# Long convolution of a two-block model: the first filter products moved to the norm ahead of it, and one residual moved by a weight chunk

## What is computed

```
x = x + gate * y                                   # y: output of the MLA layer
a = modulate(rmsnorm(x, norm_g[1]), shift, scale)  # the norm "n5"
u = depthwise_conv(a @ hy_w_in, hy_conv_w, hy_conv_b)
z, g1, g2 = channels of u
z = g1 * (longconv(z, filter 0) + bias[0] * z)
z = g2 * (longconv(z, filter 1) + bias[1] * z)
x = x + gate * ((z * silu(gate channels)) @ hy_w_out)
```

## Time and profile before

| | |
|---|---|
| three runs | 1974.87, 1975.39, 1976.33 us (median 1975.39) |
| profiled execution | 1977.09 us, its span 1975.3 us |
| granted TensorE clock, mean | 0.991 |
| PE busy | 1917.8 us (97%) |
| DVE busy | 1400.4 us (71%) |
| ACT busy | 833.0 us (42%) |
| POOL busy | 226.7 us (11%) |
| chain that ended last | PE 70%, DVE 19%, ACT 6%, issue 3% |

### The profile page before, as it was taken

How to read it: one execution, slowest core, us unless ns; L and a number is a source line. 1 busy time by engine, 2 the same in 40 slices (tenths; PEclk the granted TensorE clock), 3 DMA queues, 4 the chain that set the end, 5 groups by cost and what they waited for, 6 DMA issues and landing times.

```text
span 1975.3 us, 24342 instructions
## 1 busy us (share of the span) xinstructions
PE 1917.8 (97%) x9606; PEld 1602.5 (81%) x9606; DVE 1400.4 (71%) x2091; ACT 833.0 (42%) x1324; POOL 226.7 (11%) x233
## 2 busy tenths in 40 slices
PE   8999999999999999999999999999999989999997
PEld 6888887778788889888888888778888878788886
DVE  5477766998889678848755874556555568798884
ACT  5233334442233356644323443444434344455442
POOL 2133321002201330010000001100000101010011
PEclk9999999999999999999999999999999989999998
DMA  5212123335544431134443433321111323332421
GB/s 185 75 58 65 54 65 96 138 132 191 201 152 152 142 124 42 45 106 139 149 163 125 144 112 96 107 64 40 36 37 39 114 68 128 91 134 75 150 95 53
DMA packets 60531, 206.55 MB, mean 105 GB/s; under 512 B 6785, under 2 KB 7233, under 8 KB 59265
## 3 DMA queue, kind: packets, MB, share of 16 engines
q1 hardware_dynamic: 52864, 191.36, 29.1%
q10 hardware_dynamic: 7552, 13.64, 2.0%
HBM read 194.48 MB, written 10.49 MB: 104 GB/s over the span
## 4 chain that ended last, share of the span: by engine, by line
PE 70%; DVE 19%; ACT 6%; issue 3%; POOL 1%; DMA 0%; ACTq 0%; DVEq 0%; SPq 0%
PE PS L335 18%; PE PS L339 17%; PE PS L338 17%; DVE wlo L1899 4%; DVE col_f L2140 2%; PE PS L448 2%; PE PS L954 2%; ACT whi L1221 2%; PE PS L342 2%; PE PS L345 1%; PE PS L346 1%; PE PS L746 1%; PE PS L943 1%; DVE q L2062 1%; PE PS L727 1%
## 5 line engine op out<-in xcount | busy, mean ns | idle before, releaser
L335 PE MATMUL PS<-nhi,whi 128*128 128x512 f32 x1456 | 587.8, 404 | 16.3 <-DVE wlo L1899 4.7
L339 PE MATMUL PS<-nhi,wlo 128*128 128x512 f32 x1456 | 570.4, 392 | 0.0
L338 PE MATMUL PS<-nlo,whi 128*128 128x512 f32 x1456 | 569.3, 391 | 0.0
L1899 DVE TENSOR_TENSOR wlo<-raw,whi 128x1024 fp32r<-128x1024 f32 x288 | 362.6, 1269 | 154.2 <-ACT whi L1221 152.9
L1221 ACT ACTIVATE whi<-raw 128x1024 fp32r<-128x1024 f32 x288 | 299.7, 1052 | 167.8 <-PE PS L335 97.8
L335 PEld LDWEIGHTS PS<-nhi,whi 128*128 128x128 f32 x1456 | 275.0, 189 | 78.6 <-issue 9.7
L339 PEld LDWEIGHTS PS<-nhi,wlo 128*128 128x128 f32 x1456 | 274.4, 188 | 59.1
L338 PEld LDWEIGHTS PS<-nlo,whi 128*128 128x128 f32 x1456 | 275.4, 189 | 51.5 <-issue 1.0
L2800 POOL TENSOR_TENSOR diag<-diag,sqb 128x512 f32<-128x512 f32 (+1 forms) x56 | 72.9, 1301 | 758.6 <-ACT sqb L1230 675.8
L335 PE MATMUL PS<-hh_f,whi 128*128 128x512 f32 x352 | 137.2, 390 | 0.0
L339 PE MATMUL PS<-hh_f,wlo 128*128 128x512 f32 x352 | 137.0, 389 | 0.0
(11 more groups left out here) (371 smaller groups left out, 3285.7 us busy)
## 6 DMA issues: line engine op xcount, KB each, us to landing
raw<-in_stream SPq DMA_DIRECT2D x288, 512.0 KB, 3.5
aw_f<-in_ada SPq DMA_DIRECT2D x48, 512.0 KB, 4.5
rows<-sd_f ACTq DMA_DIRECT2D x32, 256.0 KB, 2.3
rows_h<-rows SPq DMA_DIRECT2D x8, 1024.0 KB, 6.3
wd_f<-in_decay ACTq DMA_DIRECT2D x16, 256.0 KB, 3.2
hT<-in_xT SPq DMA_DIRECT2D x8, 256.0 KB, 6.8
out<-hT SPq DMA_DIRECT2D x8, 256.0 KB, 2.0
wd_f<-in_filt_out ACTq DMA_DIRECT2D x8, 128.0 KB, 3.0
```

Source lines behind the costliest of these rows:

```text
L335: op = e.matmul(out, hi, xh, start=first, stop=False)
L338: e.matmul(out, hi, xl, start=False, stop=False)
L339: return e.matmul(out, lo, xh, start=False, stop=last)
L1899: e.tensor_tensor(m.wlo[:, c % HL, :], m.raw[:, c % RAW, :], m.whi[:, c % HL, :].bitcast(F), SUB).then_inc(*s.w_lo.tick(c))
```

## The change

The 18 products of the first six tiles (alternating row, cosine part, sine part of the first filter group) are taken in the norm n5. Six come between the two groups of one-column sums, six between the sums and the spread, six behind the spread. The row and the sine part both use bank 4 now, one after the other, with ACT's copy of the row between them; the cosine part uses bank 5. ACT copies the row behind the root, and the sine and cosine parts at the start of `forward(0)`. The counters on ACT and DVE count the six tiles at the new place. On DVE the residual of tile 7 now stands ahead of the rounding that its loop reaches with the seventh tile.

```diff
@@ summed_late (PE)
         for last, src in enumerate((m.acc, m.sqb[:, 1, :])):
             if last:
+                between()
                 q.wait_ge(*s.sq.at(site, KD - 1))
@@ hyena (PE)
-        summed_late("n5", lambda: q.wait_ge(*s.h.at("mla_out", 0)))
+
+        def first_row():
+            q.wait_ge(*s.h.at("mla_out", 2))
+            q.wait_ge(*s.made_v.at("h_lo", 0, 0, 0))
+            for x in range(2):
+                op = mm_w(B[4], tiles.take([("alt", x, 0)]), a.hh[:, 0, x, :], a.hl[:, 0, x, :], x == 0, x == 1)
+            op.then_inc(*s.filled.tick("alt", 0, 0))
+
+        def first_part(b, key, col, half, rows):
+            for k, x in enumerate(rows):
+                op = mm_w(b, tiles.take([("dft", k, col)]), a.hh[:, half, x, :], a.hl[:, half, x, :], k == 0, k == 1)
+            op.then_inc(*s.filled.tick(key, 0, 0, 0))
+
+        summed_late("n5", lambda: q.wait_ge(*s.h.at("mla_out", 0)), first_row)
+        first_part(B[5], "bk", 0, 0, (0, 1))
         spread("n5")()
+        q.wait_ge(*s.taken_a.at("alt", 0, 0))
+        q.wait_ge(*s.made_v.at("h_lo", 0, 0, 3))
+        first_part(B[4], "bj", 4, 1, (2, 3))
@@ convolve, forward(j) (PE): with j == 0 of the first group "done", its alt and dft products are left out
-                    q.wait_ge(*s.taken_a.at("alt", od, c))
+                    q.wait_ge(*(s.taken_a.at("bj", 0, 0, 0) if done else s.taken_a.at("alt", od, c)))
@@ hyena (ACT)
         root("n5")
+        for _ in range(2):
+            w.tiles(1)
+        q.wait_ge(*s.filled.at("alt", 0, 0))
+        e.activation(a.alt[:, :], B[4], ACT.Copy).then_inc(*s.taken_a.tick("alt", 0, 0))
+        for _ in range(4):
+            w.tiles(1)
@@ convolve, forward(j) (ACT)
+                if done:
+                    q.wait_ge(*s.filled.at("bj", 0, 0, 0))
+                    e.activation(ks[:, 1, :], bu, ACT.Copy).then_inc(*s.taken_a.tick("bj", 0, 0, 0))
                 e.activation(ks[:, 0, :], bk, ACT.Copy).then_inc(*s.taken_a.tick("bk", od, c, j))
@@ mla, last loop (DVE)
-            for k, _ in enumerate(w.steps(KD if i > 3 else 1)):
+            for k, _ in enumerate(w.steps(6 if i == 7 else KD if i > 3 else 1)):
                 if (i, k) in ROWS_AT:
                     next(rows)
             residual(MLA_OUT_BANKS[i], i, ("mla_out",), m.ada[0][:, 16 + i, 0:1])
+        for _ in range(2):
+            w.tiles(1)
@@ hyena (DVE)
         root("n5", m.rc)
+        for _ in range(6):
+            w.tiles(1)
```

More of the change, by code:

```diff
@@ L378, in summed, with summed_late @@
         return sums(site, m.acc, 4, ready)
-    def summed_late(site, free):
+    def summed_late(site, free, between=lambda: None):
         q.wait_ge(*s.acc.at(site, KD - 2))
@@ L1084, in forward @@
                 sums, differences = (0, 1), (2, 3)
-                if j == 0:
+                done = j == 0 and prev is None
+                if j == 0 and not done:
                     for k, x in enumerate(sums):
@@ L1088, in forward @@
                         if k == 0:
-                            q.wait_ge(*(s.taken_v.at("bu", *prev, 3) if prev else s.h.at("mla_out", 1)))
+                            q.wait_ge(*s.taken_v.at("bu", *prev, 3))
                             q.wait_ge(*s.made_v.at("h_lo", od, c, 0))
@@ L1092, in forward @@
                     op.then_inc(*s.filled.tick("alt", od, c))
-                for k, x in enumerate(sums if j < 2 else differences):
+                for k, x in enumerate(() if done else sums if j < 2 else differences):
                     w = tiles.take([("dft", k, j)])
@@ L1098, in forward @@
                         else:
-                            q.wait_ge(*(s.taken_a.at("bk", *prev, 3) if prev else s.h.at("mla_out", 2)))
+                            q.wait_ge(*s.taken_a.at("bk", *prev, 3))
                         q.wait_ge(*(s.made_v.at("hm", od, c) if j else s.made_v.at("h_lo", od, c, 0)))
                     op = mm_w(bk, w, a.hh[:, 0, x, :], a.hl[:, 0, x, :], k == 0, k == 1)
-                op.then_inc(*s.filled.tick("bk", od, c, j))
-                for k, x in enumerate(differences if j < 2 else sums):
+                if not done:
+                    op.then_inc(*s.filled.tick("bk", od, c, j))
+                if j == 0:
+                    q.wait_ge(*s.made_v.at("zt", od, c, 3))
+                for k, x in enumerate(() if done else differences if j < 2 else sums):
                     w = tiles.take([("dft", k, 4 + j)])
                     if k == 0:
-                        q.wait_ge(*(s.taken_a.at("bj", od, c, j - 1) if j else s.made_v.at("zt", od, c, 3)))
+                        if j:
+                            q.wait_ge(*s.taken_a.at("bj", od, c, j - 1))
                         q.wait_ge(*s.made_v.at("h_lo", od, c, 3))
                     op = mm_w(bj, w, a.hh[:, 1, x, :], a.hl[:, 1, x, :], k == 0, k == 1)
-                op.then_inc(*s.filled.tick("bj", od, c, j))
+                if not done:
+                    op.then_inc(*s.filled.tick("bj", od, c, j))
                 even, odd = Z_SIGNS[j]
@@ L1803, in forward @@
                 i = j % 2
-                if j == 0:
+                done = j == 0 and od == 0 and c == 0
+                if j == 0 and not done:
                     for _ in range(2):
@@ L1812, in forward @@
                     e.activation(a.alt[:, :], bu, ACT.Copy).then_inc(*s.taken_a.tick("alt", od, c))
-                w.tiles(1)
-                w.tiles(1)
+                for _ in range(0 if done else 2):
+                    w.tiles(1)
                 q.wait_ge(*s.filled.at("bk", od, c, j))
@@ L1825, in forward @@
                     e.activation(a.hh[0:1, 0, 0, :], a.hm[0:1, :], ACT.Copy).then_inc(*s.made_a.tick("hm", od, c))
-                for _ in range(2):
-                    w.tiles(1)
-                q.wait_ge(*s.filled.at("bj", od, c, j))
-                e.activation(ks[:, 1, :], bj, ACT.Copy).then_inc(*s.taken_a.tick("bj", od, c, j))
+                if not done:
+                    for _ in range(2):
+                        w.tiles(1)
+                    q.wait_ge(*s.filled.at("bj", od, c, j))
+                    e.activation(ks[:, 1, :], bj, ACT.Copy).then_inc(*s.taken_a.tick("bj", od, c, j))
                 for _ in range(Z_TILES[j]):
@@ L2668, in forward @@
                 i = j % 2
+                done = j == 0 and od == 0 and c == 0
                 if j == 0:
-                    for _ in range(4):
+                    for _ in range(0 if done else 4):
                         w.tiles(1)
@@ L2674, in forward @@
                                     SUB).then_inc(*s.made_v.tick("hm", od, c))
-                for _ in range(Z_TILES[j] + (2 if j == 0 else 4)):
+                for _ in range(Z_TILES[j] + (0 if done else 2 if j == 0 else 4)):
                     w.tiles(1)
```

## The result

| | before | changed |
|---|---|---|
| median of 14 runs each, us | 1975.75 | 1971.83 |
| lowest to highest, us | 1973.38 to 1977.18 | 1970.34 to 1973.32 |
| profiled execution, us | 1977.09 (span 1975.3) | 1970.34 (span 1968.5) |
| mean granted clock of that execution | 0.991 | 0.995 |

The ratio is 0.9981, with a 95% interval of 0.9973 to 0.9989: 3.9 us less in the medians, against 3.7 forecast. The changed kernel was run once more, beside two other kernels: 1971.67 (11 runs, before 1975.08 in 17), ratio 0.9979 [0.9970, 0.9987].

What follows compares the result with a forecast made beforehand. TensorE is busy for 97% of the span, so edits pay only where it waits, runs at half clock or ends a chain. 1.62 + 1.37 - 1.13 + 1.85 = 3.7 us, from 1975.39 to 1971.7; range 1969.5 to 1975.0.

Steps and rivals of the forecast that it cites:

- Step 1: On DVE, the last residual goes ahead of a weight chunk, so the square ends 1.15 us earlier.
- Step 2: Six row products between the groups of sums spend the residual's gain but for 0.08 us; root 0.6 us earlier.
- Step 3: Six cosine products between sums and spread, hidden but for 0.03 us; spread takes 1.02, scaled rows start 1.62 us earlier.
- Step 4: Six sine products behind the spread and two ACT copies, all hidden; products end near 1589.0, stream starts at 1590.48.
- Step 5: Start of the projection stream at full clock: nine steps take 1.90 us and not 3.27, 1.37 us gained.
- Step 6: At the turn, one more chunk ahead of DVE's four folds stalls PE's transposes by 1.13 us.
- Step 7: At the convolution's start ACT runs through behind the last column: 1.85 us gained, 0.72 net of the stall.
- B: No stall at the turn: gain 4.8 us, time 1970.6; chance 0.16.
- E: ACT's copies behind the last column do not run through: gain 1.9 us, time 1973.5; chance 0.05.
- C: Clock falls once in the norm, at about 1585, for 3.3 us: gain 2.1 us, time 1973.3; chance 0.16.
- D: Half clock through the whole chain of the norm: 0.4 us slower, time 1975.8; chance 0.06.
- two bounds: Trace before the change: full clock after 2.63 us without products near 1272, half clock following 2.06 us near 1682.

Runs made afterwards that it cites:

- the four edits together: Changed kernel plus a chunk ahead of the first take, ACT's copies ahead of the last, DVE's chunk and row's low half in its wait: 1968.81 us, ratio 0.9966.

## Why the prediction was right

**Step 1, the residual**: 0.43 behind the last MLA product, as forecast (1.15 us). **Step 2**: the square is ready at 1581.50 (1580.87 + 0.63), 1.2 us before the six row products are through, and the second group starts behind them, at 3.02 against 3.04 before. That it spends what step 1 wins is shown from two sides: with the residual alone the sums start at 1.90, and with the products alone the sums don't move (3.04). The group took 0.95 (forecast 1.03), the root came 0.62 earlier (0.6). One reading of this step was wrong: the forecast gives the residual 0.08 us in the change, and it is worth 0.30 at the root and 0.28 at the first multiply, since without it the root follows ACT's table load of 1.28 us, which the forecast does not count. The sum is not touched by it, as in the change the load ends 0.86 ahead of the root. **Step 3**: the cosine products are hidden and the spread takes 1.07 (1.02): 1.57 us for 1.62. **Step 4**: six products and ACT's copy are hidden; PE still has 1.42 idle ahead of the stream (about 1.5). **Step 5**: 1.33 us for 1.37 (the gain at the first take, 2.89, less the 1.56 at the start of the stream).

**Step 6**: PE's idle piece is 0.91, less than the 1.13 forecast, but three of the four transposes stand ahead of it and only the last waits. From the first transpose to the next product it is 1.48 us (1625.87 - 1624.39) against 0.37 before, 1.11 more, and so it is from the first take to the last one (26.86 against 25.75). The term should be read from such distances, not from the idle piece alone. Moving the chunk away gives it back (25.73).

**Step 7**: the multiply comes 4.85 behind the take, forecast 4.95, before 6.80: 1.95 us for 1.85. ACT copies without a pause. PE's wait is 1.94 (1.9), and costs next to nothing in the first multiply: with the copies ahead of the take the wait is gone, and that multiply gains only 0.2.

The sum of the steps is 3.73 at the first multiply, for 3.7. It is that close partly by luck, since the errors of 0.02 to 0.10 have both signs.

**The rivals.** B (no stall) falls by the 1.11 us. E (the copies do not run through) falls by ACT's timeline. C and D (the clock falls in the chain) did not happen in either profile of the change. Here the forecast was right on grounds that were thinner than it made them: it argued from twelve long products and no wait above 1.5 us, and the experiments show how near it was. Its two bounds were single draws. The waits of 2.63 us at 1272 and of 2.06 us at 1682 stand in all thirteen profiles, the first in a part of the program that all kernels share. The first was followed by half clock in five of them, three times with the very next product, as here with the copies ahead of the last take (before: 0.47):

```profile
1275.33 0.77 PE L335 MATMUL PS<-nhi,whi 128*128 128x512 f32 x1 [2.63 <-DVE call L2465]
```

The second was followed by it in eight. So the row at 1275.01 was no bound, and that the clock would stay up in the change did not follow from it. In the norm itself, of all thirteen profiles:

| what stands between the last MLA product and the spread | clock fell in the norm |
|---|---|
| sums and waits only (before, residual alone, all behind the spread) | 3 of 3 profiles |
| six products behind the sums | 2 of 4 |
| six products between the two groups of sums, six behind them | 0 of 6 |

The Trainium skill (TensorE: Matmul & The Clock Gate, "What's actually happening") says that "the default state is throttled, and activity releases the throttle". The traces agree in direction: the more long products in the chain, the rarer the fall, and none where there were twelve. If the order made no difference, three falls among the nine profiles of the first and last row would all be in the first row once in 84 times, so the products probably have a part in it. Whether their number does it or their place between the sums isn't shown: no kernel has six between the sums and none behind. The prediction says that the trace disagrees with the page, since the wait at 1272 did not make the clock fall. That doesn't follow from the sentence quoted, which names no length of a wait, and in five of thirteen profiles it did fall there. The traces also show that D's price is real: in the order with six products behind the sums and a late residual it took the whole gain of the chain and 0.07 us more (8.06 against 7.99). D's chance of 0.06 for the change itself is not contradicted by its two profiles, nor by the four others with six products between the sums.

What the timed runs can settle is less: the ratio of each experiment has an interval of about 0.1% on either side, 2 us. That the change is faster than before, and that the four edits together are faster than before by 0.21 to 0.47%, is shown by times; with the products behind the spread no difference from before is shown (0.9983 to 1.0002). The sizes of single terms are shown by the traces alone.

## What to carry to other kernels

In a chain of short operations on several engines PE's waits can take products that are wanted later; put them where they also end in time at half clock, because a product ahead of a link costs nearly twice as much once the clock has fallen (0.43 against 0.23 us a step here). Take from one trace that a wait can pass at full clock, not that it always will. After moving work out of one place, follow each engine's order to the next place where it has no slack: here the tiles taken ahead brought a chunk in front of the folds (1.1 us), and the copies freed ACT only to leave DVE as the end of the chain. Cost each term from rows of the trace and compare by distances between events, since two executions of the same kernel differ by more than such a change gives (17 of the kernel before: 1972.44 to 1978.77). Look for what runs beside the step that you shorten: here a table load of 1.28 us was hidden until the sums ahead of it got faster.

## What the runs showed of the hardware

- Whether the granted clock falls behind a given wait differs from execution to execution of the same work. Behind 2.63 us without a product (start of the wait near 1272) it fell in 5 of 13 profiles, behind 2.05 to 2.10 us (near 1680) in 8 of 13.
- In the norm, with six products behind the sums, it fell in two of four, at 1584.4 and 1585.3. The moved residual doesn't decide it: one of the two that fell has it, and both that stayed.
- ACT loads its function table for the root for 1.28 us, as soon as the square ahead of it is done. With the residual late and the sums at full clock the root starts at the end of that load (products alone: 0.01 us behind it).
- The new wait of 1.94 us ahead of the turned rows was followed by half clock in two of the seven profiles that have it. In that of the change six products begin over 2.69 us (1639.48 to 1642.17) where six steps at full clock take 1.37. The forecast left this cost out. DVE's multiply was not later for it: 60.97 in both profiles of the change, one with it and one without.
- A group of one-column sums takes 0.95 to 1.05 us at full clock, but the next product starts 0.80 to 0.92 us behind its start.
